# Later turns and norms, split mixtures and softmax, and a shorter chain to the first gather in a hybrid decoder step

## The reference

```python
n  = rms_norm(x, g_mix);  z = n @ w_in                    # 4608 columns
u, va, qb, kb, vb, qm = split(z)                          # gelu on u, va; norms on va, qb, kb, qm per head
ya = u * (tril(w_s) @ va + b_s)                           # 4 groups of 128, chunks of 128
yb = dilated window attention(qb, kb, vb)                 # 16 heads of 64, three windows, the sample against 2048 cached rows
ym = softmax(qm @ mk.T / sqrt(128)) @ mv                  # mk, mv = 256 memory tokens @ w_mem_kv (cached for the sample)
h  = x + concat(ya, yb, ym) @ w_out
t  = rms_norm(h, g_ffn)
grp = argmax(t @ w_rg)                                    # 1 of 4 groups
top_v, top_i = top_k(t @ w_re[grp], 2)                    # 2 of 8 experts in it
y  = h + sum over the two: softmax(top_v) * (silu(t @ w_gate[e]) * (t @ w_up[e])) @ w_down[e]
```

## Time and profile before

| | |
|---|---|
| median of 3 runs | 1235.33 us (1233.87 to 1235.64) |
| the profiled execution's own time, its span | 1235.69 us, 1233.9 us |
| TensorE matmul busy, weight load busy | 1087.9 us (88%), 601.8 us (49%) |
| VectorE, ScalarE, POOL busy | 529.3 us (43%), 209.0 us (17%), 40.4 us (3%) |
| granted TensorE clock, mean | 0.949 |
| moved by DMA | 385.48 MB, mean 312 GB/s |
| chain that ended last: PE, DMA, DVE, issue | 64%, 18%, 10%, 3% |

### The profile page before, as it was taken

The page is one execution under the profiler, slowest core; times in us unless marked ns, Lnnn a source line. Parts: engine busy times, 40 slices in busy tenths (PEclk is TensorE's granted clock), DMA queues, the critical chain, the costliest instruction groups (busy, mean ns, idle before and its releaser), DMA issues.

```text
span 1233.9 us, 17375 instructions
## 1 busy us (share of the span) xinstructions
PE 1087.9 (88%) x7143; PEld 601.8 (49%) x7143; DVE 529.3 (43%) x1012; ACT 209.0 (17%) x433; POOL 40.4 (3%) x38
## 2 busy tenths in 40 slices
PE   8969889898999999999999995998978797888876
PEld 3657666664666666667667642333322232222222
DVE  4384354364354445474354305343424233242323
ACT  1111011131122212231101103212111111111110
POOL 0030110001010000010000000000000000000000
PEclk9889889998999999999989997999999999999998
DMA  9996225797898997851474333999999999999994
GB/s 330 359 256 257 103 94 221 315 343 286 331 364 337 389 373 291 341 218 69 167 296 182 144 151 137 418 428 425 426 430 427 427 429 428 427 429 425 427 425 173
DMA packets 38751, 385.48 MB, mean 312 GB/s; under 512 B 4879, under 2 KB 7567, under 8 KB 10223
## 3 DMA queue, kind: packets, MB, share of 16 engines
q1 hardware_dynamic: 36112, 376.87, 76.6%
q0 software_dynamic: 1568, 5.62, 1.7%
q10 hardware_dynamic: 1008, 2.10, 0.5%
HBM read 376.67 MB, written 7.90 MB: 312 GB/s over the span
## 4 chain that ended last, share of the span: by engine, by line
PE 64%; DMA 18%; DVE 10%; issue 3%; ACT 3%; POOL 1%; SPq 0%; DVEq 0%; ACTq 0%; POOLq 0%
PE ps L583 21%; DMA arena<-w_gu 14%; PE ps L575 6%; PE ps L990 6%; PE ps L973 5%; PE ps L1020 5%; PE ps L1004 3%; PE ps L777 3%; DMA arena<-w_proj 3%; PE ps L565 3%; PE ps L744 3%; PE ps L997 2%; DMA arena<-w_o 1%; PE ps L1025 1%; PE ps L760 1%
## 5 line engine op out<-in xcount | busy, mean ns | idle before, releaser
L583 PE MATMUL ps<-arena 128*128 128x256 f32 x1456 | 351.8, 398 | 3.7 <-DMA arena<-w_o 2.8
L583 PEld LDWEIGHTS ps<-arena 128*128 128x128 f32 x1456 | 283.8, 199 | 59.8 <-issue 17.6
L990 PE MATMUL ps<-arena,cst 128*32 128x512 f32 x1024 | 132.2, 651 | 38.6 <-DMA arena<-w_gu 37.3
L1705 DVE STREAM_TRANSPOSE cst<-ps 128x512 f32<-128x512 f32 x31 | 22.2, 717 | 196.3 <-PE ps L973 196.3
L973 PE MATMUL ps<-arena 128*32 128x512 f32 (+1 forms) x768 | 98.0, 625 | 6.5 <-DVE arena L1680 6.5
L575 PE MATMUL ps<-arena 128*64 128x256 f32 x832 | 101.3, 385 | 0.0
L990 PEld LDWEIGHTS ps<-arena,cst 128*32 128x32 f32 x1024 | 33.1, 116 | 130.8 <-issue 87.5
L1004 PE MATMUL ps<-arena,cst 128*32 128x512 f32 x512 | 65.8, 634 | 20.7 <-DVE cst L1707 20.7
L575 PEld LDWEIGHTS ps<-arena 128*64 128x64 f32 x832 | 55.1, 136 | 38.3 <-issue 14.8
L1273 DVE TENSOR_TENSOR arena<-arena 128x512 f32<-128x512 f32 x52 | 35.7, 687 | 76.9 <-PE ps L583 52.6
L1723 DVE COPY arena<-ps 32x512 f32<-32x512 f32 x64 | 44.2, 691 | 49.7 <-PE ps L1004 48.7
(11 more groups left out here) (255 smaller groups left out, 962.0 us busy)
## 6 DMA issues: line engine op xcount, KB each, us to landing
arena<-w_gu SPq DMA_DIRECT2D x64, 2048.0 KB, 32.1
arena<-w_dn SPq DMA_DIRECT2D x32, 2048.0 KB, 31.3
arena<-w_proj SPq DMA_DIRECT2D x43, 1024.0 KB, 7.6
arena<-kc SPq DMA_DIRECT2D x16, 2048.0 KB, 9.2
arena<-vc SPq DMA_DIRECT2D x16, 2048.0 KB, 9.2
arena<-w_o SPq DMA_DIRECT2D x16, 1024.0 KB, 4.9
arena<-kc SPq DMA_DIRECT2D x8, 1024.0 KB, 8.1
arena<-vc SPq DMA_DIRECT2D x8, 1024.0 KB, 9.8
```

Of the source, the lines that this page charges most:

```text
L583: last = mm(psum[:, regions(v)[j - 1]], left[a], right[:, a], start=first and opens and a == 0, stop=final and a == 1, skip_group_check=True)
L990: last = mm(ps[g:g + 32, 0, :], xgT[:, s % 2, kt, :], gate_up[(3 * s + h) % RING][:, k, :], start=kt < 4, stop=kt >= KT - 4)
```

## The change

What it does, by place. **Steps:** the first norm moves from step 0 to 5, the first twelve turns by 3 to 6 steps. **SP:** the quarters of `xT` are spread between pieces 4, 5, 6; piece 47 is issued before the waits for the gate and the memory heads and before x, gains and constants. **VectorE, start:** each `x_quarter` stands behind one `mix_weights`; the means of the squares (`ms_ready`, which POOL waits for) stand behind `mix_weights(7)` instead of before it. **Mixtures:** `mix_weights` is two halves; in the steps the first stands at s % 3 = 1, the second at s % 3 = 2. **Sample softmax:** a maximum for each part as it comes, one of the three, three exponentials, a sum of three; TensorE's turn j waits for its own part. **Routing:** experts of other groups are pushed down by -3e38 and searched among 32 at once, so two operations go; the slot of a first block is found from the rank alone (`eid32`, `late`), before totals and block lists; the gather stands ahead of `routed`; five more matmuls (`keep_busy`) stand around the ranks; the softmax of the two weights moves behind the first transpose, ahead of and behind `blocks_ready`.

```diff
@@ -58,8 +58,8 @@
-NORM_AT = (0, 12, 24, 48, 60, 84, 96)
-TURN_AT = [3, 4, 5, 6, 15, 16, 17, 18, 27, 28, 29, 30, 61, 61, 62, 62, 63, 63, 64, 64, 88, 89, 90, 91]
+NORM_AT = (5, 12, 24, 48, 60, 84, 96)
+TURN_AT = [9, 10, 11, 12, 18, 19, 20, 21, 30, 31, 32, 33, 61, 61, 62, 62, 63, 63, 64, 64, 88, 89, 90, 91]
@@ -399,9 +402,15 @@
-            for i in (4, 5):
-                sp.wait_ge(unit_done, 2 * (i - 2))
-                weights(i)
+            def x_columns(q):
+                k = slice(q * K4, (q + 1) * K4)
+                sp.dma_start(xT[:, k], x_t[:, k]).then_inc(s_xt[q], 16)
+            sp.wait_ge(unit_done, 4)
+            weights(4)
+            x_columns(0)
+            sp.wait_ge(unit_done, 6)
+            weights(5)
@@ -412,11 +421,11 @@
             x_tile(1)
+            x_columns(1)
             sp.wait_ge(unit_done, 8)
             weights(6)
-            for q in range(QTR):
-                k = slice(q * K4, (q + 1) * K4)
-                sp.dma_start(xT[:, k], x_t[:, k]).then_inc(s_xt[q], 16)
+            x_columns(2)
+            x_columns(3)
             x_tile(2)
@@ -488,6 +497,8 @@
+            sp.wait_ge(unit_done, UNITS_M + UNITS_X + 3)
+            weights(47)
             sp.wait_ge(gate_y, G)
@@ -506,7 +517,7 @@
-            for o in range(13):
+            for o in range(1, 13):
@@ -753,7 +764,7 @@
-                pe.wait_ge(sexp, n + 1)
+                pe.wait_ge(sexp, 3 * n + j + 1)
@@ -958,11 +969,17 @@
+            def keep_busy(n):
+                for _ in range(n):
+                    mm(ps[:, 5, :], ident, cst[:, 0:512], start=True, stop=True)
+            keep_busy(3)
             pe.wait_ge(onehots, 1)
...
             mm(ps[:, 4, 0:32], c("ones"), acc[:, 2], start=True, stop=True).then_inc(ranks, 1)
+            keep_busy(2)
@@ -1026,10 +1043,10 @@
+            pe.wait_ge(n2_ready, 3)
+            gather(0, 1)
             pe.wait_ge(routed, 1)
             last_body = pe.value_load(cnt_i[0:1, 0:1], min_val=NEXP // BODY - 1, max_val=NBLK // BODY - 1)
-            pe.wait_ge(n2_ready, 3)
-            gather(0, 1)
@@ -1123,7 +1140,9 @@
                 act.wait_ge(smx, n + 1)
-                nc.scalar.activation(sc_s, sc_s, ACT.Exp, bias=st_m[:, 10:11], accum_out=st_l[:, 10:11]).then_inc(sexp, 1)
+                for j in range(3):
+                    nc.scalar.activation(sc_s[:, PART[j]], sc_s[:, PART[j]], ACT.Exp, bias=st_m[:, 10:11],
+                                         accum_out=st_sums[:, j:j + 1]).then_inc(sexp, 1)
@@ -1263,7 +1282,7 @@
-            def mix_weights(i):
+            def mix_first(i):
@@ -1274,6 +1293,11 @@
                 V.tensor_tensor(wmix[:, 2], b22, b12, ALU.subtract).then_inc(w_mixed, 1)
+            def mix_second(i):
+                m, u = 4 * (i - 4), 3 * (i - 5)
+                b11, b12, b21, b22 = w_blocks(i)
                 if m:
@@ -1283,6 +1307,10 @@
+            def mix_weights(i):
+                mix_first(i)
+                mix_second(i)
             def add_products(v, out):
@@ -1308,22 +1336,28 @@
-            mix_weights(5)
-            mix_weights(6)
-            dve.wait_ge(sumsq, 5)
-            V.tensor_scalar(stat[:, 0:5], stat[:, 0:5], 1.0 / D, EPS, ALU.mult, ALU.add).then_inc(ms_ready, 1)
-            mix_weights(7)
-            for q in range(QTR):
+            def x_quarter(q):
                 dve.wait_ge(s_xt[q], 16)
...
                 mix_tokens(xT, x_mix, q, x_mixed)
-                if q == 0:
-                    add_products(0, quarters(mv))
-                    add_fourth(0, quarters(mv))
-                    mix_weights(8)
+            mix_weights(5)
+            x_quarter(0)
+            mix_weights(6)
+            x_quarter(1)
+            mix_weights(7)
+            dve.wait_ge(sumsq, 5)
+            V.tensor_scalar(stat[:, 0:5], stat[:, 0:5], 1.0 / D, EPS, ALU.mult, ALU.add).then_inc(ms_ready, 1)
+            x_quarter(2)
+            add_products(0, quarters(mv))
+            add_fourth(0, quarters(mv))
+            mix_weights(8)
+            x_quarter(3)
@@ -1433,12 +1467,16 @@
                 last.then_inc(s_used, 1)
-                if j == 2:
-                    dve.wait_ge(s_used, 3 * n + 3)
-                    V.tensor_reduce(st_m[:, 10:11], sc_s, X, ALU.max, negate=True).then_inc(smx, 1)
+                dve.wait_ge(s_used, 3 * n + j + 1)
+                if j < 2:
+                    V.tensor_reduce(st_part[:, j:j + 1], sc_s[:, PART[j]], X, ALU.max)
+                else:
+                    link(V.tensor_reduce(st_part[:, j:j + 1], sc_s[:, PART[j]], X, ALU.max))
+                    V.tensor_reduce(st_m[:, 10:11], st_part, X, ALU.max, negate=True).then_inc(smx, 1)
             def sample_rec(n):
-                dve.wait_ge(sexp, n + 1)
+                dve.wait_ge(sexp, 3 * n + 3)
+                link(V.tensor_reduce(st_l[:, 10:11], st_sums, X, ALU.add))
                 V.reciprocal(st_r[:, 10:11], st_l[:, 10:11]).then_inc(srec, 1)
@@ -1556,7 +1594,9 @@
                 if s % 3 == 1:
-                    mix_weights(9 + s // 3)
+                    mix_first(9 + s // 3)
+                if s % 3 == 2:
+                    mix_second(9 + s // 3)
@@ -1624,20 +1664,17 @@
-            link(V.tensor_tensor(goh, iota[:, 0:4].unsqueeze(1).to_broadcast([P, 3, 4]), grp.to_broadcast([P, 3, 4]), ALU.is_equal))
-            link(V.tensor_tensor(prod, lg[:, :, 4:36].rearrange("p t (g e) -> p t g e", g=4),
-                                 goh.unsqueeze(3).to_broadcast([P, 3, 4, 8]), ALU.mult))
-            link(V.tensor_reduce(esel, prod.rearrange("p t g e -> p t e g"), X, ALU.add))
+            link(V.tensor_tensor(goh, iota[:, 0:4].unsqueeze(1).to_broadcast([P, 3, 4]), grp.to_broadcast([P, 3, 4]), ALU.not_equal))
+            link(V.scalar_tensor_tensor(prod, goh.unsqueeze(3).to_broadcast([P, 3, 4, 8]), -3e38,
+                                        lg[:, :, 4:36].rearrange("p t (g e) -> p t g e", g=4), ALU.mult, ALU.add))
             for t in range(3):
-                last = V.max(top[:, t, :], esel[:, t, :])
+                last = V.max(top[:, t, :], prod[:, t].rearrange("p g e -> p (g e)"))
             link(last)
             for t in range(3):
-                last = V.max_index(ti[:, t, :], top[:, t, :], esel[:, t, :])
+                last = V.max_index(ti[:, t, :], top[:, t, :], prod[:, t].rearrange("p g e -> p (g e)"))
             link(last)
-            link(V.tensor_copy(tif, ti[:, :, 0:2].rearrange("p t k -> p k t").unsqueeze(3)))
             for m, ts in ((P, slice(0, 2)), (64, slice(2, 3))):
-                last = V.scalar_tensor_tensor(eid[0:m, :, ts], grp[0:m, ts].unsqueeze(1).to_broadcast([m, 2, ts.stop - ts.start, 1]), float(EPG),
-                                              tif[0:m, :, ts], ALU.mult, ALU.add)
+                last = V.tensor_copy(eid[0:m, :, ts], ti[0:m, ts, 0:2].rearrange("p t k -> p k t").unsqueeze(3))
             link(last)
@@ -1646,25 +1683,36 @@
             V.tensor_tensor(acc[:, 2], acc[:, 1], asum[:, 2], ALU.add).then_inc(onehots, 1)
-            dve.wait_ge(rs_ready, state["n"])
-            link(V.tensor_tensor(w1p, top[:, :, 1:2], top[:, :, 0:1], ALU.subtract))
-            V.tensor_tensor(dd, w1p, st_hr[:, 0:3].unsqueeze(2), ALU.mult).then_inc(route_d, 1)
+            V.tensor_scalar(eid32, eid, float(SLOTS), 1.0, ALU.mult, ALU.add)
+            def one_hots():
+                return V.tensor_tensor(own, iota1.unsqueeze(1).unsqueeze(1).to_broadcast([P, 2, 3, P]), sid.to_broadcast([P, 2, 3, P]), ALU.is_equal)
             dve.wait_ge(ranks, 1)
+            link(V.tensor_tensor(pick, moh, ps[:, 3, 0:96].rearrange("p (t e) -> p t e", t=3).unsqueeze(1).to_broadcast([P, 2, 3, 32]), ALU.mult))
+            link(V.tensor_reduce(rankf, pick, X, ALU.add))
+            V.tensor_scalar(late, rankf, float(SLOTS), 4096.0, ALU.is_ge, ALU.mult)
+            link(V.tensor_tensor(posf, rankf, eid32, ALU.add))
+            link(V.tensor_tensor(sid, posf, late, ALU.add))
+            link(one_hots())
+            V.tensor_tensor(pm, own[:, 0], own[:, 1], ALU.add).then_inc(p_made, 1)
             V.tensor_copy(tot, ps[:, 4, 0:32])
-            link(V.tensor_tensor(pick, moh, ps[:, 3, 0:96].rearrange("p (t e) -> p t e", t=3).unsqueeze(1).to_broadcast([P, 2, 3, 32]), ALU.mult))
-            V.tensor_tensor(cmp, tot.unsqueeze(2).to_broadcast([P, 32, NTHR]), thr.unsqueeze(1).to_broadcast([P, 32, NTHR]), ALU.is_gt)
-            link(V.tensor_reduce(rankf, pick, X, ALU.add))
-            V.tensor_reduce(more, cmp, X, ALU.add)
             link(V.tensor_tensor(geq, rankf.to_broadcast([P, 2, 3, NTHR]),
                                  thr.unsqueeze(1).unsqueeze(1).to_broadcast([P, 2, 3, NTHR]), ALU.is_ge))
-            V.tensor_tensor_scan(incl, more, zer, 0.0, ALU.add, ALU.add)
+            V.tensor_tensor(cmp, tot.unsqueeze(2).to_broadcast([P, 32, NTHR]), thr.unsqueeze(1).to_broadcast([P, 32, NTHR]), ALU.is_gt)
```

(21 more changed lines are left out.)

7 lines of the change are left out of this document (5 added, 2 removed).

## The result

The changed kernel takes 1200.09 us (median of 4 runs, 1198.15 to 1201.7) against 1234.6 for the kernel before in the same comparison: a ratio of 0.9723, 95% interval 0.9699 to 0.9746. The profiled execution took 1201.35 us, its span is 1199.5 (1233.9 before).

The account below looks back on a forecast made before the run. The prediction took the end to be `blocks_ready` + 437 + 26.6 us. Its terms summed to -23.5, taking 1235.7 to 1212.2, and with the median 0.4 below the profiled run to 1212 us; range for 8 in 10: 1202 to 1226.

Parts of the forecast that it names:

- What bounds the kernel: Whole span: the end is `blocks_ready` + 437 us of expert weight stream + 26.6 us to the span's end.
- First turn, +4.5: Before x unit 3: later stores delay weight piece 11 by 1.7 us, landing at 107.9; +4.5 us, from -12.4 to +5.6.
- Second and third norm, -2.2: Steps 15 to 18, 27 to 30: wait moves from turn to mixed products; 1.1 us won per norm, bounds 0 and -14.8.
- Sample softmax, -12: Eight sample steps: softmax in parts shortens TensorE's waits for the exponential; -12 us, bounds -4 and -17.
- Mixtures elsewhere, -3.9: Waits at 532.41, 556.81 and 591.36: 1.3 us less on VectorE before each; -3.9 us, bounds -1 and -8.
- Piece 47, -5.9: Before 620.82: earlier issue removes the 2.8 us wait and 3.0 of half clock; -5.9 us, at least -2.8.
- Routing, -4.0: Router to `blocks_ready`: shorter chain of small operations; -5.2 us at full clock (6 in 10), -2.4 at half, -4.0 taken.
- piece 11 was not in time: Rival before x unit 3: DMA slack lets piece 11 land in time, -12.4 instead of +4.5, total 1195; chance 0.08.
- the softmax's gain was not taken by the next dependency: Rival in the sample steps: next dependency takes the gain, softmax -4, other short waits -1, norms 0, total 1225; chance 0.17.
- the second half of the mixtures was not late: Slower rival: `mix_second` comes late in 33 later x units, 1.4 us each, +46, total 1258; chance 0.05.
- The likeliest case: Whole kernel: the summed terms hold, 1212 us; chance 0.70, own range 1205 to 1219.
- All five signs: Over 10 us before unit 3; stalls near 126, 170; no piece 47 wait; exponential waits below 4; `blocks_ready` 437 before last piece.

Follow-up runs that it names:

- piece 11 first: Changed kernel with weight piece 11 issued once its slot is free, ahead of the bias rows and the keys: 1193.98 us (ratio 0.9665).
- the late keys: Changed kernel, weight piece 11 issued early, mixtures ahead of second and third norm, sample step 0's keys issued behind pieces 13, 14, 15: 1175.59 us (0.9536).

## Why the prediction was off, step by step

- **What bounds the kernel** (list of the blocks + 437 + 26.6): right, within 0.3 us for the last piece and 0.9 for the tail.
- **First turn, +4.5:** the step was right in kind (TensorE waits 11.5 us for piece 11 in place of 10.05 for the turn; the wait moved, as forecast) and too dear: unit 3 ends at 117.7, not 119.1, mostly because piece 11 landed 0.75 us later and not 1.7; the rest is that only two of the four turns ran before its end. I had derived the delay from the issue time, and that itself was short: the stores start 4.7 us later, not 2.8. By the rule cited from the Trainium skill (DMA: Bandwidth & Descriptors, section "Issuing engines are not separate DMA queues"), as I applied it, it would have been all of the stores' delay; the trace, 0.75 us for stores 4.7 us late, does not bear that out. That transfers of all queues share the engines is not contradicted by it: the engines were full in that stretch (share 1.00 from 86 to 107 us of the changed kernel), what stood ahead of piece 11 was the same, and only taking the keys away from ahead of it (piece 11 first) brought it in time.
- **Second and third norm, -2.2:** right; -2.6 between the small units at 120.9 and 211.8 us of before, and the waits stand before L594, where the text put them. It is the split's, as the text said: alone, with the turns where they were, the split wins 2.7 us up to 211.8.
- **Sample softmax, -12: the failed step.** What failed is that it stood for all that the change wins in the sample steps, -19.3. The text gave the split mixtures a place there in step 0 alone, and so left most of its gain out; the runs show -7.5 for the split in these steps alone and -9.1 undone, as much as the softmax, which by itself was sized too large (-7.3 alone, -8.8 undone). Together they won 16.4. The remaining 2.9 are luck: clock behind a wait of 3.56 us that is the same in both kernels, which nothing in the text could foresee. I looked for the split's gain under waits that name VectorE, and all of its idle time was in waits that name the exponential or another operation of ScalarE, which itself stands behind VectorE's queue.
- **Mixtures elsewhere, -3.9:** the same fault, smaller: -5.8; the three waits gave 1.0, 1.8 and 3.0, of which 3.5 is clock. The second did not get shorter: it moved to the transposes right behind (1.25 us before, 1.37 after), and what it gave is clock alone. By the medians the whole split is worth 20 to 21 us; by the trace of the split alone it is 22.6, of which 6.0 are clock behind the padded queries and behind piece 47, where it shortened no wait by more than 0.1. Its pieces in the text make 10.
- **Piece 47, -5.9:** -5.9 came, but half of it by luck. Only the wait, some 3 us, belongs to the edit in every run; the half clock behind it is in the trace of before and in none of the three others with a late piece 47.
- **Routing, -4.0:** -5.3. Full clock at the gather, to which I gave 6 in 10, is what came, and the five matmuls are why. On that branch the text had -5.2. The reason it gave, that the rows show the clock lost only behind 2.07 us or more, is not good: behind the wait of 1.25 before 556.81 the 16 matmuls that took 3.62 in the changed kernel ran at half clock too:

```profile
558.42 5.30 PE L583 MATMUL ps<-arena 128*128 128x256 f32 x16
```

- **The rivals:** piece 11 was not in time; the softmax's gain was not taken by the next dependency; the second half of the mixtures was not late. The likeliest case was the right one, with the split's part of its largest term left out; its own range, 1205 to 1219, took in only the landing, the clock at the gather and the softmax, and 1202 lay just below that. All five signs that the text named for being right came true: they tested the path, and none of them the size of the term that failed.

## What to carry to other kernels

An operation that an engine does in order delays everything behind it in its queue, so price a move or a split at every wait whose releaser sits behind that queue, not only at waits that name the operation. A wait that is shortened, and not removed, can still give back its whole stretch of half clock, or none of it; compare busy times of the same matmuls to see that part, over several traces, before an edit is credited with it. When a wait for a transfer appears in a stretch where the DMA engines are full, move bytes that are needed late behind it, and look at the next piece too: here one piece moved ahead only handed the wait on, and the late keys were what removed it.
